# Other start addresses for the moving operands: 1,280-byte rows of h, and filler tensors ahead of h, g and y

## What is computed

```python
for l in range(2):                                   # first block
    x = x + 0.5 * swiglu(rms_norm(x), wg, wu, wd)    # 1024 -> 2816 -> 1024
    z = rms_norm(x) @ w_in                           # q, k, v and three conv parts
    x = x + concat(sliding_window_attention, short_conv) @ w_out
    x = x + 0.5 * swiglu(rms_norm(x), wg, wu, wd)
x = rms_norm(x)
h = concat(meta_tokens, x)                           # second block
p = rms_norm(h) @ w_in_2                             # latents, gates, q, k, v
y = concat(latent_attention, neighbourhood_attention) * silu(gates)
h = h + y @ w_out_2
```

## The kernel before

| tensor | bytes | start, less that of w_hi | remainder by 512 | by 256 |
|---|---|---|---|---|
| w_hi (four slots of 5,632) | 22,528 | 0 | 0 | 0 |
| w_lo | 22,528 | 22,528 | 0 | 0 |
| h_hi (8 rows of 272 x 4 = 1,088) | 8,704 | 45,056 | 0 | 0 |
| h_lo | 8,704 | 53,760 | 0 | 0 |
| g_hi, g_lo (22 rows of 1,024 each) | 22,528 | 99,072; 121,600 | 256 | 0 |
| y_hi, y_lo (16 rows of 1,024; second block, in the place of g) | 16,384 | 99,072; 115,456 | 256 | 0 |

## Time and profile before

### The profile page before, as it was taken

One profiled execution on the slowest core, in us unless ns is written; L12 is line 12 of the kernel. 1 busy time (PEld: TensorE's weight loads), 2 busy tenths in 40 slices (PEclk: granted clock), 3 DMA queues, 4 the chain that ended last, 5 costly groups with the idle time before them and its releaser, 6 DMA issues.

```text
span 1277.3 us, 27436 instructions
## 1 busy us (share of the span) xinstructions
PE 1242.1 (97%) x10050; PEld 1203.8 (94%) x10050; DVE 822.1 (64%) x1388; ACT 656.3 (51%) x1121; POOL 170.6 (13%) x228
## 2 busy tenths in 40 slices
PE   6999999999999999999999999999997999998998
PEld 6999999899999999999999999999996887998888
DVE  6766654868666655666655767666656666645664
ACT  5545543546444545444543645454544665655652
POOL 3000000351000000000000351000000000401960
PEclk9999999999999999999999999999997999999999
DMA  8555753435555654555644445556642430543542
GB/s 283 186 190 184 236 162 131 145 124 190 187 182 195 225 159 141 185 183 195 224 162 136 133 134 186 195 181 205 204 159 74 134 128 20 166 149 125 174 149 83
DMA packets 56742, 210.91 MB, mean 165 GB/s; under 512 B 7200, under 2 KB 9280, under 8 KB 56544
## 3 DMA queue, kind: packets, MB, share of 16 engines
q1 hardware_dynamic: 54048, 203.45, 48.0%
q0 software_dynamic: 2480, 6.48, 1.7%
q10 hardware_dynamic: 144, 0.06, 0.0%
HBM read 208.91 MB, written 1.05 MB: 164 GB/s over the span
## 4 chain that ended last, share of the span: by engine, by line
PE 95%; ACT 2%; DVE 1%; issue 1%; DMA 0%; ACTq 0%; DVEq 0%; SPq 0%
PE bank L1145 28%; PE bank L1147 28%; PE bank L1146 28%; PE bank L1183 2%; PE bank L1488 2%; PE bank L1468 1%; ACT w_hi L448 1%; PE bank L1453 1%; PE bank L1390 1%; PE bank L1392 1%; PE bank L1391 1%; PE bank L1448 1%; PE bank L1238 0%; PE bank L1237 0%; PE bank L1247 0%
## 5 line engine op out<-in xcount | busy, mean ns | idle before, releaser
L1145 PE MATMUL bank<-h_hi,w_hi 128*128 128x256 f32 (+1 forms) x1992 | 570.2, 286 | 16.5 <-DVE w_lo L731 11.8
L1146 PE MATMUL bank<-h_lo,w_hi 128*128 128x256 f32 (+1 forms) x1992 | 562.9, 283 | 0.0
L1147 PE MATMUL bank<-h_hi,w_lo 128*128 128x256 f32 (+1 forms) x1992 | 562.8, 283 | 0.0
L731 DVE TENSOR_TENSOR w_lo<-w_raw,w_hi 128x1024 fp32r<-128x1024 f32 (+1 forms) x360 | 466.7, 1298 | 87.0 <-ACT w_hi L448 86.3
L448 ACT ACTIVATE w_hi<-w_raw 128x1024 fp32r<-128x1024 f32 (+1 forms) x360 | 397.3, 1107 | 97.1 <-PE bank L1147 75.6
L1145 PEld LDWEIGHTS bank<-h_hi,w_hi 128*128 128x128 f32 x1992 | 378.4, 190 | 25.2 <-issue 21.2
L1147 PEld LDWEIGHTS bank<-h_hi,w_lo 128*128 128x128 f32 x1992 | 378.9, 190 | 0.0
L1146 PEld LDWEIGHTS bank<-h_lo,w_hi 128*128 128x128 f32 x1992 | 376.4, 189 | 0.9
L1145 PE MATMUL bank<-g_hi,w_hi 128*128 128x256 f32 x832 | 235.6, 283 | 0.3 <-DVE x_res L916 0.3
L1146 PE MATMUL bank<-g_lo,w_hi 128*128 128x256 f32 x832 | 235.4, 283 | 0.0
L1147 PE MATMUL bank<-g_hi,w_lo 128*128 128x256 f32 x832 | 235.4, 283 | 0.0
(11 more groups left out here) (160 smaller groups left out, 1217.9 us busy)
## 6 DMA issues: line engine op xcount, KB each, us to landing
w_raw<-in_w SPq DMA_DIRECT2D x296, 512.0 KB, 3.3
w_raw<-in_wd SPq DMA_DIRECT2D x64, 704.0 KB, 4.1
w_raw<-in_relbias POOLq DMA_DIRECT2D x64, 64.0 KB, 2.3
btab_sb<-in_btab POOLq DMA_DIRECT2D x1, 1536.0 KB, 9.9
x_res<-in_xT SPq DMA_DIRECT2D x2, 512.0 KB, 5.0
out_T<-x_res SPq DMA_DIRECT2D x8, 128.0 KB, 1.7
rope_sb<-in_rope POOLq DMA_DIRECT2D x1, 272.0 KB, 3.8
mats_sb<-in_mats POOLq DMA_DIRECT2D x1, 192.0 KB, 3.9
```

Source lines behind the costliest of these rows:

```text
L731: dve.tensor_tensor(wlo[:, slot, 0:cols], raw[:, slot, 0:cols], whi[:, slot, 0:cols].bitcast(F32), ALU.subtract).then_inc(lo_ready[slot], 1)
L1145: pe.matmul(o, h, xh, start=first, stop=False)
L1146: pe.matmul(o, h, xl, start=False, stop=False)
L1147: return pe.matmul(o, lo, xh, start=False, stop=last)
```

## The change

Rows of h grow from 272 to 320 elements (1,280 bytes), and three filler tensors that nothing reads or writes move what is declared behind them: 48 elements ahead of h_hi, 64 ahead of g_hi, 32 ahead of y_hi. All that reads or writes h or the latents uses the new row length.

```diff
+HS = TM + 48
...
-        hhi = sb("h_hi", [P, KT * TM], F32R)
-        hlo = sb("h_lo", [P, KT * TM], F32R)
+        sb("h_hi_phase", [P, 48])
+        hhi = sb("h_hi", [P, KT * HS], F32R)
+        hlo = sb("h_lo", [P, KT * HS], F32R)
...
+            sb("g_hi_phase", [P, 64], F32, first)
             ghi = sb("g_hi", [P, FT, T], F32R, first)
...
+            sb("y_hi_phase", [P, 32], F32, second)
             yhi = sb("y_hi", [P, 16 * T], F32R, second)
...
-        QL0 = 2 * TM
+        QL0 = 2 * HS
         KEYS = (0, BLK, TM - BLK)
-        latw = {"kv": (0, TM), "ql": (QL0, T)}
+        latw = {"kv": (0, TM, HS), "ql": (QL0, T, T)}
...
-                act.activation(hhi[:, bass.ds(k * TM, T)], h32[:, slot, 0:T], ACT.Copy).then_inc(h_hi, 1)
+                act.activation(hhi[:, bass.ds(k * HS, T)], h32[:, slot, 0:T], ACT.Copy).then_inc(h_hi, 1)
...
-                h = bass.ds(k * TM, T)
+                h = bass.ds(k * HS, T)
...
-                return hhi[:, k * TM:k * TM + n], hlo[:, k * TM:k * TM + n]
+                return hhi[:, k * HS:k * HS + n], hlo[:, k * HS:k * HS + n]
...
-                        c = src + i * wid
+                        c = src + i * step
...
-                        c = latw["kv"][0] + i * TM + KEYS[tt]
+                        c = latw["kv"][0] + i * HS + KEYS[tt]
```

More of the change, by code:

```diff
@@ L472, in norm @@
                     act.wait_ge(h32_done, q * KT + k + 1)
-                    act.activation(hhi[:, k * TM:k * TM + n], h32[:, k % 4, 0:n], ACT.Copy).then_inc(h_hi, 1)
+                    act.activation(hhi[:, k * HS:k * HS + n], h32[:, k % 4, 0:n], ACT.Copy).then_inc(h_hi, 1)
             def high(q, k, slot):
                 act.wait_ge(h32_done, q * KT + k + 1)
-                act.activation(hhi[:, bass.ds(k * TM, T)], h32[:, slot, 0:T], ACT.Copy).then_inc(h_hi, 1)
+                act.activation(hhi[:, bass.ds(k * HS, T)], h32[:, slot, 0:T], ACT.Copy).then_inc(h_hi, 1)
             def late_rstd(q):
@@ L663, in projections @@
                             act.wait_ge(pj_taken, st["n0"] + i + 1)
-                            off, wid = latw[kind]
-                            act.activation(yhi[:, off + k * wid:off + (k + 1) * wid], h32[:, c, 0:wid],
+                            off, wid, step = latw[kind]
+                            act.activation(yhi[:, off + k * step:off + k * step + wid], h32[:, c, 0:wid],
                                            ACT.Copy).then_inc(h_hi, 1)
@@ L761, in norm @@
                         dve.wait_ge(h_hi, q * KT + k)
-                        c = (k - 1) * TM
+                        c = (k - 1) * HS
                         dve.tensor_tensor(hlo[:, c:c + n], h32[:, (k - 1) % 4, 0:n], hhi[:, c:c + n].bitcast(F32),
@@ L1009, in projections @@
                             c = st["latent"][i]
-                            off, wid = latw[kind]
+                            off, wid, step = latw[kind]
                             dve.wait_ge(h_hi, 8 * KT + c + 1)
-                            dve.tensor_tensor(ylo[:, off + k * wid:off + (k + 1) * wid], h32[:, c, 0:wid],
-                                              yhi[:, off + k * wid:off + (k + 1) * wid].bitcast(F32), ALU.subtract)\
+                            dve.tensor_tensor(ylo[:, off + k * step:off + k * step + wid], h32[:, c, 0:wid],
+                                              yhi[:, off + k * step:off + k * step + wid].bitcast(F32), ALU.subtract)\
                                .then_inc(h_lo, 1)
@@ L1358, in run @@
                 elif kind in ("kn", "qn", "qpe"):
-                    src, wid = latw["kv" if kind == "kn" else "ql"]
+                    src, wid, step = latw["kv" if kind == "kn" else "ql"]
                     if k % 4 == 0:
```

## The result

The changed kernel takes **1250.22 us**, the median of four runs from 1245.3 to 1253.66; the kernel before, in the same series, took 1278.2 (1276.44 to 1280.1). The ratio is 0.9771, with a 95% interval of 0.9752 to 0.979: 28 us are gone where 45.7 were forecast. The change's runs lie 8.4 us apart, those of before 3.7.

A forecast was written before the change was run, and what follows sets the result against it. TensorE, busy 97% of the span, was taken as the bound, stalled by the moving operand's offset modulo 256. Terms -21.1, -16.6, -5.9, -1.1 and -1.0 sum to -45.7 us, giving 1234 us, range 1219 to 1268.

The forecast's parts named there:

- the offsets do nothing: All streams: 118.3 against 120.0 ns comes from order of work or piece length; 1280 us, chance 0.05.
- only g: If 512 counts, h never repeats an offset and stays at 118.3 ns; g alone gains 16.6 us; 1262 us, chance 0.11.
- slow lock: Offset 192 held falls to 120 ns as 0 does; h loses 9.5 us, g gains nothing; 1289 us, chance 0.16.
- an attracting state of 113.3 ns would do that: At offset 192, streams of h and g fall into a repeating 113.3 ns step, ended only by work in between.
- middle lock: The state at 192 is a cycle of unequal steps, mean 117.5 ns; 12 us less, 1267 us, chance 0.08.
- six matmuls on k tile 7: Trace before, 209.09 to 209.80: mean 118 ns, read as beginning badly but ending in the same state as the fast triples.
- gate_up, 4224: Four gate_up stages, 4224 matmuls on h: from 118.3 to 113.3 ns each, -21.1 us.
- g, 2496: 2496 matmuls on g: from 120.0 to 113.3 ns each, -16.6 us.
- other h, 1488: 1488 other 256-column matmuls on h, in runs of 24: five reach the state, 19/24 gain 5.0 ns, -5.9 us.
- y, 456: 456 matmuls on y, at offset 64: a step of about 117.6 ns, -1.1 us (-3.1 to +0.5).
- 272 columns, 504: 504 matmuls with 272 columns: -2 ns each, -1.0 us (-3.4 to +1.0).
- Fillers, cover and gaps at 0: Fillers, row length and addresses add no instruction, wait or bytes; cover stays; waits between stages don't shrink: 0.

The follow-up runs named there:

- rows-only kernel: Changed kernel with all fillers removed, rows of 1,280 bytes kept, so h, g and y lie at 0 modulo 256: 1289.77 us.
- nine-matmul kernel: Changed kernel plus nine unread matmuls, three each at 0, 64 and 128 modulo 256, behind each gate_up's norm sum: 1245.59 us.

## Why the prediction was right, and where its size was off

**The direction and the cause.** The prediction had the step depend on the moving operand's offset modulo 256. That stood: without the fillers 120.0 ns, with them 113.3 or 117.8, same instructions. It also had this offset count against the weights that are loaded meanwhile, and called it a stall in feeding the array; the weights stayed in their place in all runs, so neither is shown. The rivals fall with it: *the offsets do nothing* (1280) by every run above; *only g* (1262) because h too reached 113.3, and g at 448 behaves as at 192; *slow lock* (1289) for offset 192, though the price was exact for the offset 0: 1289 was forecast for a held 120 ns, and the rows-only kernel took 1289.77. Against *the offsets do nothing* the prediction said that a step has no other reason to vary than the offsets; it has one, as pairs 3 and 4, fast in one execution and slow in the other at equal addresses, show.

**The step that failed** is "an attracting state of 113.3 ns would do that". Offset 192 has a second stable state, 117.8 ns, that ends no more by itself than the fast one. It is the *middle lock* rival (117.5 ns) and the forecast in one kernel, drawn at each restart. The evidence I used couldn't show it: in the kernel before, a stream that restarted behind the norm's sum came to 192 only by way of k tiles at 0, 64 and 128. The six matmuls on k tile 7 were read rightly: their steps 117, 117, 118, 122, 118, 114 are the way to 113.3 ns, as the nine-matmul kernel shows. What failed is the step from there to every stream: behind a restart the same offset can settle at 117.8 instead. All fast would be some 1246.2 - 6.9 = 1239.3 us of span, 1241 with the 1.8 around it; all slow is 27.7 more, about 1269, near the rival's 1267 (1268 by its own sum: 12 less than 1279.9). The forecast of 1234 lies under the lower end.

**The terms**, in the profiled execution:

| term | forecast | measured there |
|---|---|---|
| gate_up, 4224 | -21.1 | 3 stages x 1056 x 5.0 = -15.8, one x 1056 x 0.55 = -0.6: -16.4 |
| g, 2496 | -16.6 | 3 x 528 x 6.67 = -10.6, 528 x 2.2 = -1.2, and about -1 on wout's 384, some at 117.8: -12.8 |
| other h, 1488 | -5.9 | runs of 24 from 118.1 to 115.2, the two long runs in qkv stay at 117.8: about -3.7 |
| y, 456 | -1.1 | 119.6 to 117.8: -0.8 |
| 272 columns, 504 | -1.0 | 126.0 to 123.5: -1.3 |
| sum | -45.7 | -35.0 |

The span fell by 31.1. Most of the 4 us between is found by setting the two traces side by side, matmul by matmul. The steps that grew or shrank by over 25 ns add up to +3.4 us:
- +1.5 in the first piece of pair 3, at a granted clock of 0.50 as shown above, and +0.7 in that of pair 1 and the norm's sum behind it, where the full clock came 1.4 us later than before (at 17.7 us of the span, before at 16.3);
- about +1.2 around three short waits that weren't there before, each of 0.22 or 0.23 us of idle time and ended by VectorE (`x_res` in the first wout, `h_lo` in the first pieces of pairs 2 and 4);
- about +1.0 in waits and norm steps between stages and around a later half-clock stretch of the second block, and -1.2 at its start, where the half-clock stretch ended earlier.

PE's idle time rose by 0.8 us in all (35.2 to 36.0), mostly in the three waits. The prediction had no term for the clock and took the waits as unchanged; both errors are small, and the clock's part has no visible tie to the change. The estimates for y and for 272 columns were good to half a microsecond, although neither had a row. For y that is luck: its 117.8 is one of the two steps of offset 64, which can also have 113.3, as h showed there. *Other h* failed for the same reason as gate_up: a run of 24 either settled at 113.3 or stayed at 117.8 to its end.

**Fillers, cover and gaps at 0** stood. The wait for `w_lo` is 11.7 us against 11.8, and VectorE is busy for 71% of a fast gate_up window (forecast 73%), DMA for 0.60 (0.61).

**The range** held the time, but its upper end came from the two rivals and not from a mixture, so that it reached far enough is partly luck. A forecast with the mixture in it, half the pairs slow, would have been 1241 + 2 x 6.9 = 1255.

## What to carry to other kernels

If TensorE is busy all the time and still takes longer for a matmul than its columns, compare streams that differ only in the address of an operand, and write down the offsets of the moving operand modulo 256; padding rows and fillers added no instruction here and cost nothing to try. Don't hold an offset before its value is known: here one held value cost 10 us and another gave 28. And look at a steady stream in two or three executions: a state picked at the start of a stage shows in the step of each stage, more clearly than in the times of the runs (1245.3, 1248.0, 1252.44 and 1253.66 here), and a few useless instructions ahead of the stage can be worth their time.

## What the runs showed that was not expected

- **Two stable speeds of one instruction stream**, 113.33 and 117.78 ns a matmul at offset 192 or 64, kept over some 1,560 matmuls (180 us) and a change of operand from h to g; at a held offset nothing but a wait ended one in these traces. Offset 160 has two also, 117.3 and 118.7.
- **The choice isn't fixed by the program** and falls at the restart behind the norm's sum, and nine matmuls at 0, 64 and 128 between it and the stream made the fast one come up in 4 stages of 4 in the profile and in five even runs; three and six did not hold it. The way in was the same in all long stages in which a stream came to 192 from 0, 64 and 128 without a wait (four with the nine matmuls, four with the fillers alone): five steps of 116 to 124 ns, then 113.3.
- **The map by offset is not smooth**: 120.0, 116.7, 113.3 or 117.8, 120.0, 118.7, 117.3 or 118.7, 113.3 or 117.8, 118.3 ns for 0 to 224 in steps of 32.
- **At half the clock it is gone**, after as before. The kernel after at the second block's start, timeline of PE:
```profile
947.07 0.43 PE L1150 MATMUL bank<-h_lo,w_hi 128*128 128x272 f32 x1
947.29 0.43 PE L1151 MATMUL bank<-h_hi,w_lo 128*128 128x272 f32 x1
947.52 0.43 PE L1149 MATMUL bank<-h_hi,w_hi 128*128 128x272 f32 x1
947.75 0.43 PE L1150 MATMUL bank<-h_lo,w_hi 128*128 128x272 f32 x1
947.97 0.43 PE L1151 MATMUL bank<-h_hi,w_lo 128*128 128x272 f32 x1
```
  Four steps take 0.90 us, 225 to 227 ns each, as in the earlier trace rows, at 272 columns and a granted clock of 0.50. At full speed the same shape went from 126.0 to 123.5 ns.

**Open**: what makes the offset count, whether it counts against the weights' place (no run moved them), what in the restart picks the state (no run varied the restart's timing), and whether a shorter lead-in that begins at 0 would do.
